# Two halves of the adaLN product placed apart in each turn, weight loads reordered, and two output tiles with their banks exchanged

## The reference

```
mod = jax.nn.silu(c) @ w_ada + b_ada
sh1, sc1, g1, sh2, sc2, g2 = jnp.split(mod, 6, axis=-1)
h = rmsnorm(x, norm_pre1) * (1 + sc1[:, None]) + sh1[:, None]
proj = h @ w_in
bg, cg, ua, q, k, v, r, lr, ga, gb = jnp.split(proj, split_idx, axis=-1)
conv_out, conv_buf_new = causal_dwconv(cg * ua, conv_buf, conv_w, conv_b)
y_a = bg * conv_out
o, gla_state_new = gla_recurrence(q, k, v, log_a, gla_state)
y_b = o.reshape(Bn, T, GLA_HEADS * GLA_DV) * jax.nn.silu(r)
merged = jax.nn.sigmoid(ga) * y_a + jax.nn.sigmoid(gb) * y_b
x = x + g1[:, None] * rmsnorm(merged @ w_out, norm_post1)
```

## Time and profile before

| | |
|---|---|
| median of 3 executions | 976.56 us (972.80 to 977.62) |
| the profiled execution | 974.86 us |
| its span, first to last instruction | 973.1 us |
| mean granted TensorE clock | 0.997 of full |
| PE busy | 947.2 us, 97% of the span |
| DVE busy | 623.8 us, 64% |

### The profile page before, as it was taken

One profiled execution on the slowest core, in us unless ns is written; L12 is line 12 of the kernel. 1 busy time (PEld: TensorE's weight loads), 2 busy tenths in 40 slices (PEclk: granted clock), 3 DMA queues, 4 the chain that ended last, 5 costly groups with the idle time before them and its releaser, 6 DMA issues.

```text
span 973.1 us, 18387 instructions
## 1 busy us (share of the span) xinstructions
PE 947.2 (97%) x7479; PEld 859.7 (88%) x7479; DVE 623.8 (64%) x924; ACT 458.1 (47%) x771; POOL 170.8 (18%) x101
## 2 busy tenths in 40 slices
PE   5999999999899998999999999999999999999997
PEld 4889999878789888899898889999999999888886
DVE  3687777311588785436438589999999898660204
ACT  4565545534234234543463356556655556633212
POOL 3010000363224234223344000000000000012430
PEclk9999999999999999999999999999999999999999
DMA  9754843843867679746527041233333332422212
GB/s 335 242 79 91 111 88 67 194 131 44 128 192 205 146 204 168 115 99 153 134 95 227 1 122 52 66 104 93 87 94 103 90 106 66 129 66 87 87 52 97
DMA packets 133509, 115.57 MB, mean 119 GB/s; under 512 B 9946, under 2 KB 110066, under 8 KB 133426
## 3 DMA queue, kind: packets, MB, share of 16 engines
q1 hardware_dynamic: 133329, 114.37, 46.7%
q10 hardware_dynamic: 96, 0.04, 0.0%
HBM read 107.02 MB, written 7.35 MB: 118 GB/s over the span
## 4 chain that ended last, share of the span: by engine, by line
PE 86%; DVE 6%; issue 4%; ACT 2%; POOL 1%; DMA 1%; DVEq 0%; ACTq 0%; POOLq 0%
PE pair L2508 30%; PE pair L2415 23%; PE pair L2583 14%; PE pair L2853 5%; PE pair L2405 2%; PE pair L2638 1%; PE pair L2665 1%; POOL w_lo L977 1%; PE pair L2345 1%; PE pair L2730 1%; PE pair L2719 1%; PE pair L2575 1%; PE pair L2576 1%; DVE w_lo L2060 1%; PE pair L2577 1%
## 5 line engine op out<-in xcount | busy, mean ns | idle before, releaser
L977 POOL TENSOR_TENSOR w_lo<-raw,w_hi 128x1024 fp32r<-128x1024 f32 x41 | 103.5, 2526 | 613.0 <-ACT w_hi L1052 496.8
L2415 PE MATMUL pair<-h_hi,w_hi 128*128 128x288 f32 x624 | 145.2, 306 | 2.3 <-DVE ext L1843 1.9
L2415 PE MATMUL pair<-h_lo,w_hi 128*128 128x288 f32 x624 | 138.9, 296 | 3.5 <-issue 3.5
L2415 PE MATMUL pair<-h_hi,w_lo 128*128 128x288 f32 x624 | 139.3, 296 | 0.7 <-issue 0.7
L2415 PEld LDWEIGHTS pair<-h_hi,w_hi 128*128 128x128 f32 x624 | 101.9, 189 | 13.3 <-issue 10.8
L1052 ACT ACTIVATE w_hi<-raw 128x1024 fp32r<-128x1024 f32 x54 | 56.8, 1056 | 107.6 <-PE pair L2577 70.7
L2415 PEld LDWEIGHTS pair<-h_hi,w_lo 128*128 128x128 f32 x624 | 102.4, 189 | 4.5 <-issue 4.5
L2508 PE MATMUL pair<-h_hi,w_hi 128*128 128x288 f32 x348 | 102.8, 295 | 0.0
L2508 PE MATMUL pair<-h_hi,w_lo 128*128 128x288 f32 x348 | 102.4, 294 | 0.0
L2508 PE MATMUL pair<-h_lo,w_hi 128*128 128x288 f32 x348 | 102.3, 294 | 0.0
L2415 PEld LDWEIGHTS pair<-h_lo,w_hi 128*128 128x128 f32 x624 | 102.2, 189 | 0.0
(11 more groups left out here) (397 smaller groups left out, 2115.2 us busy)
## 6 DMA issues: line engine op xcount, KB each, us to landing
raw_c<-in_w_ada SPq DMA_DIRECT2D x32, 512.0 KB, 5.5
raw<-in_w_in SPq DMA_DIRECT2D x96, 128.0 KB, 3.4
raw<-in_w_up SPq DMA_DIRECT2D x24, 512.0 KB, 3.8
raw<-in_w_down SPq DMA_DIRECT2D x22, 512.0 KB, 3.7
raw_up<-in_w_up SPq DMA_DIRECT2D x20, 512.0 KB, 3.8
ada_first<-in_w_ada SPq DMA_DIRECT2D x16, 512.0 KB, 9.8
raw_c<-in_w_in SPq DMA_DIRECT2D x128, 64.0 KB, 4.1
raw<-in_w_in SPq DMA_DIRECT2D x128, 64.0 KB, 3.5
```

Of the source, the lines that this page charges most:

```text
L977: pool.tensor_tensor(lo, raw_tile(n)[:, :], hi.bitcast(F32), ALU.subtract).then_inc(S("w_lo_done"), 1)
L2415: ins = pe.matmul(bank[pair][:, half, 0:HALF], w[:, i, :], x[:, i, HALF * half:HALF * half + HALF], start=i == 0 and p == 0, stop=i == KT ...
```

## The change

It has four edits. In the value stage V1's load stands before the third conv tile's, and V2's before the fourth's. In the conv stage SP issues two conv tiles and then four adaLN tiles, where it issued two adaLN tiles ahead of each conv tile. On PE the first adaLN pair of a turn stands behind the second half tile (e = 3) and the second behind the fourth (e = 7). In the gate stage the first two tiles exchange their bank pairs, and the waits for them follow. No instruction is added or taken away.

```diff
+    def c2_pair(h, e):
+
+        return (e + 1) % 2 if h == 0 and e < 2 else e % 2
...
-            for n in range(8):
+            def load_v(n):
                 load_raw(TILE_V + n, v_w[n % 4, :, :, 512 * (n // 4):512 * (n // 4) + 512])
-                if n < 2:
-                    load_c1(TILE_C1 + 2 + n)
-                elif n < 6:
+
+            load_v(0)
+            load_v(1)
+            load_c1(TILE_C1 + 2)
+            for n in range(2, 8):
+                load_v(n)
+                if n == 2:
+                    load_c1(TILE_C1 + 3)
+                if n < 6:
...
-            for i in range(4, 2 * KT + 4):
+            for i in range(4, 2 * KT + 4, 2):
+                for r in (i, i + 1):
+                    if r < 2 * KT:
+                        load_c1(TILE_C1 + r)
+                    else:
+                        load_c2(r - 2 * KT)
                 if i >= 6:
-                    load_ada(2 * i - 8)
-                    load_ada(2 * i - 7)
-                if i < 2 * KT:
-                    load_c1(TILE_C1 + i)
-                else:
-                    load_c2(i - 2 * KT)
+                    for x in range(2 * i - 8, 2 * i - 4):
+                        load_ada(x)
...
-                    elif e == 7:
-                        ada_pair(2 * j)
-                        ada_pair(2 * j + 1)
+                    elif e % 4 == 3:
+                        ada_pair(2 * j + e // 4)
...
                         if h == 0 and e < 2:
-                            pe.wait_ge(S("u_done"), 3 * KT - 3 * e)
+                            pe.wait_ge(S("u_done"), 3 * KT - 3 + 3 * e)
+                        elif h == 0 and e == 2:
+                            pe.wait_ge(S("sgb_done"), 1)
+                        elif h == 0:
+                            pe.wait_ge(S("silu_r"), 1)
...
-                    channel_tile(kc(w_hi[n % 4]), kc(w_lo[n % 4]), e % 2, (h_hi, h_lo), part=f % 2)
+                    channel_tile(kc(w_hi[n % 4]), kc(w_lo[n % 4]), c2_pair(h, e), (h_hi, h_lo), part=f % 2)
```

More of the change, by code:

```diff
@@ L1309, in sigmoid_r @@
                         act.wait_ge(S("u_done"), 3 * KT)
-                    act.activation(halves(buf_a[:, :]), out2(0), ACT.Sigmoid).then_inc(S("sr_done"), 1)
+                    act.activation(halves(buf_a[:, :]), out2(c2_pair(h, 2 * e)), ACT.Sigmoid).then_inc(S("sr_done"), 1)
                 def sigmoid_b(e):
@@ L1315, in sigmoid_b @@
                         act.wait_ge(S("gb_used"), 2 * h + e)
-                    act.activation(halves(buf_b[:, :]), out2(1), ACT.Sigmoid).then_inc(S("sgb_done"), 1)
+                    act.activation(halves(buf_b[:, :]), out2(c2_pair(h, 2 * e + 1)), ACT.Sigmoid).then_inc(S("sgb_done"), 1)
                 sigmoid_r(0)
@@ L1953, in silu @@
                         dve.wait_ge(S("m_lo_done"), j - 1)
-                    dve.tensor_tensor(halves(gated[e]), out2(0), halves(buf_a[:, :]), ALU.mult).then_inc(S("silu_r"), 1)
+                    dve.tensor_tensor(halves(gated[e]), out2(c2_pair(h, 2 * e)), halves(buf_a[:, :]), ALU.mult).then_inc(S("silu_r"), 1)
                 silu(0)
```

## The result

The changed kernel takes 996.77 us in the median of four executions (994.29 to 999.60), the kernel before beside it 976.09 us: 1.0219 times as long, 95% interval 1.0193 to 1.0245. The forecast was 984.0 us, at most 989.5: the sign was right, and the rise forecast was less than half of the one measured. The profiled execution took 994.29 us, with a span of 992.6 us against 973.1 us.

What follows compares the result with a forecast made beforehand. The prediction took PE's long list of matmuls as the bound, so only PE's stand-stills and lower clock count. From 974.86 us, + 10.91 − 2.95 + 1.53 − 0.4 gave 983.95, so 984.0 us, range 979.5 to 989.5.

Steps and rivals of the forecast that it cites:

- The loop: Conv turns 2 to 7: PE's e = 3 pair waits for DVE's copy, DVE for `mod_back`; cost 10.91 us.
- DVE's chain in turns 2 and 3: From `mod_back` to the end of DVE's copy: 11.68 us, making these turns 19.80 us each.
- The clock: In the turns, waits of 1.8 to 2.4 us at the pair would leave PE's clock alone; no cost there.
- the third rival: The clock falls in the waits of turns 2 to 6 too, 1.53 us each: 991.7 us; chance 0.06.
- The last wait's fall: At the last `mod_back`, one wait of 3.51 us brings PE's clock down; cost 1.53 us, or 0.
- the loop's term: From `mod_back` of turn 1 to that of turn 7: 114.36 us against 103.45, cost 10.91 us.
- Turn 1 and the loads: Reordered conv loads end the 3.49 us gap and its lower clock; `mod_back` of turn 1 comes 2.95 us earlier.
- 0.4 for the value stage: V1 and V2 land earlier, so PE's wait for POOL in the value stage goes; gain 0.4 us, or 0.
- the second rival: The conv-stage gap stays, being no late refill or because loads crowd again: 989.0 us; chance 0.12.
- The banks: Start of gate stage: waits of 1.92 and 0.60 us become one of 3.51; the exchange itself gains 0.
- The first rival: DVE's chain shortens to 9.29 us or less after `mod_back`, so the pair never waits: 969.7 us; chance 0.04.

Runs made afterwards that it cites:

- pairs_back: The changed kernel with both adaLN pairs of a turn on e = 7 again, loads and banks as changed: 969.50 us, 0.9927 times the kernel before.
- smp_last: The changed kernel with DVE's short product of the sample rows moved behind the copy to rows_ada: 985.88 us, 1.0101 times the kernel before.
- warm: The changed kernel with PE repeating the score item ahead of the waiting pair on e = 3, in turns 2 to 6: 1029.15 us.
- banks_only: The kernel before with the two gate-stage tiles in each other's bank and nothing else changed: 976.87 us, 1.0008 times the kernel before.
- pairs_only: The kernel before with the adaLN pairs of a turn on e = 3 and e = 7 and nothing else changed: 995.78 us, 1.0204 times.
- pool_late: The changed kernel with POOL's subtraction for the eighth and later conv tiles waiting for DVE's copy to rows_ada: 977.40 us, 1.0019 times the kernel before.

## Why the prediction was right and wrong

**The loop: right in kind.** Seven waits at the pair, one at the last `mod_back`, turns tied to DVE's chain. In turns 4, 6 and 7 the length was 18.86 us against the forecast 18.69.

**DVE's chain in turns 2 and 3: the step that failed.** "Turns 2 and 3 become 11.68 + 0.06 + 0.93 + 7.13 = 19.80 us each" took DVE's 11.68 over from the kernel before. It measured 13.82 and 13.81: 4.27 us in all. Two things went wrong. "DVE works without a pause" was read from its busy time, which counts standing still for POOL as work; the 12.33 us of turn 2, noted and set aside with 0.65, was already this effect. The timeline of the kernel before shows `level_queries` in turns 1 and 2, alone and beside POOL, and `take_mod` (line 664) behind the second, 1.19 us after `mod_back` instead of 0.52 as in turn 1:

```profile
264.77 1.36 DVE L621 TENSOR_TENSOR qd<-qd,q 128x1152 f32<-128x1152 f32 x1 [0.99 <-ACT qd L535]
...
282.21 2.41 POOL L977 TENSOR_TENSOR w_lo<-raw,w_hi 128x1024 fp32r<-128x1024 f32 x1 [5.86 <-ACT w_hi L1052]
283.30 2.53 DVE L621 TENSOR_TENSOR qd<-qd,q 128x1152 f32<-128x1152 f32 x1 [1.55 <-ACT qd L535]
285.76 0.18 DVE L664 TENSOR_TENSOR mod<-pair,prm 128x36 f32<-128x36 f32 x1
```

And the chain's length depends on where POOL starts in it, which one pair less behind `mod_back` moved by 0.85 us (11.34 in pairs_back, 10.49 in the changed kernel).

**The clock: the second step that failed.** The forecast put the clock in the turns at nothing, since "waits of 1.8 to 2.4 us are nearer to the 1.92 that left the clock alone." With the waits of 4.5 us that sentence no longer applied, but it was wrong on its own range too: a wait of 1.83 us brought the clock down in turn 5, and one of 2.25 in smp_last. Three falls of 1.5 to 1.6 make 4.64 us; the third rival had 1.53 for each, the right price at too small a chance. The last wait's fall was forecast.

**The rest of the loop's term.** A single pair and its changes of operation cost 0.14 to 0.16 us a turn more than taken, 0.92 in six turns. 4.31 (the chains of all six turns) + 4.64 + 0.92 = 9.87. The remaining 0.5 us between the forecast span of 982.2 and 992.6 lie in turn 1 (0.30 less gained) and behind turn 7 (0.17 more). The median then lies 2.5 us above the profiled execution.

**Turn 1 and the loads: right in the sum.** `mod_back` stood 3.05 us earlier, forecast 2.95 and 0.4 for the value stage. The gap is gone wherever the new order of the loads is in, with one exception: warm has a gap of 3.64 us in a half tile of turn 1, ahead of the code that it adds, in a stretch in which the DMA engines are 0.95 to 0.98 busy:

```profile
267.07 0.61 PE L2426 MATMUL pair<-h_hi,w_hi 128*128 128x288 f32 x1 [3.64 <-issue]
```

So the second rival is out for the changed kernel, but the new order doesn't rule such a gap out. That the gaps are late refills of instructions was argued in the prediction; the traces, which record the packets of the instruction queue, bear it out. This is that queue in the kernel before, from 258 to 260 us (packets, MB, share of the 16 engines):

```profile
q8 instruction: 1, 0.02, 3.3%
```

The packet, of 16 KiB, moves from 258.47 to 259.53, inside the gap, and PE goes on at 260.81, 1.28 us after the packet's end. The same holds for all thirteen "issue" gaps of 0.7 us and more (two in the kernel before, one each in banks_only and pairs_only, nine in warm): PE goes on 1.22 to 1.50 us after the end of such a packet. What makes a packet late stays open; full DMA engines are not needed for it, as warm's repeats show.

The Trainium skill (Runtime: NRT & Kernel Launch, Instruction fetch mechanics) holds that such refills are mostly hidden. The traces agree for most packets: in the kernel before 57 of 59 pass without such a gap of PE. The other two cost 3.49 us with the DMA engines full and 0.71, so the prediction's reading, that by "mostly hidden" the gap would not be a late refill, asked too much of the word.

**The banks: right.** The two waits became one of 3.42 us, forecast 3.51, and the clock fell behind it. With both pairs ahead of it the single wait is 2.57 us, and there the exchange cost nothing that can be measured (banks_only).

**The first rival** needed a chain of at most 9.29 us. pool_late comes near it with 9.5 to 10.6 and lands 0.19% above the kernel before (interval 0.08 to 0.30%), not at 969.7: 5.2 us of waits at the pairs, 3.4 at the last `mod_back` and the fall of the clock behind that are left. What the prediction held against this rival, that DVE is busy all the way, was the same misreading: the chain of 11.13 us in turns 3 to 5 measured 9.53 once POOL was out of its way.

## What to carry to other kernels

Before you hang a busy engine's chain into the path of another, compare the same operation's times across turns (least against most): where a small operation takes 2 us in one turn and 0.2 in another, its busy time hides a wait, and a shift of less than 1 us on a third engine can switch that on or off. Price a stall of PE with the clock that it may bring down behind it: here 1.5 us, behind some of the waits of 1.8 to 2.6 us and behind every one of 3 us and more in these stages. And test edits apart that came together: here the loads gained 0.7%, the pairs cost 2%, and the banks paid only once another operation, the last copy, was out of the way.

## What the runs showed of the hardware

A fall of the clock is not decided by the length of the wait alone. Waits of 1.83 us in turns 4 and 5 of the changed kernel left it alone and brought it down; the wait of 2.57 us at the last `mod_back` left it alone in pairs_back and brought it to 0.50 in banks_only:

```profile
374.00:376.00 2.00, 2.00 (x47) 1.98 (x36) 2.00 (x1) 1.38 (x3) 2.00 (x1) 1.00 0.93 89
```

```profile
380.00:382.00 2.00, 2.00 (x10) 2.00 (x10) 2.00 (x2) 1.48 (x3) 2.00 (x1) 0.50 0.91 116
```

The first is pairs_back, the second banks_only, each the stretch behind that wait. What decides between the two stays open. And DVE and POOL hold each other in both directions: POOL's subtraction takes 2.39 us in pool_late, where DVE's chain is done, and 3.00 in the changed kernel, where DVE is in the midst of it.
